# An output projection by token tiles, and an up projection in two halves of 128 tokens

## The reference

```python
y = odd_mixer(...)            # q, k, v; attention; then @ w_out_c  (1024 x 1024)
h = h + gt_m * rms_norm_2(y, g_post_m)
f = conv_ffn(modulate(h, g_pre_f, sh_f, sc_f), w_up, conv_w, conv_b, w_down)
h = h + gt_f * rms_norm_2(f, g_post_f)

def conv_ffn(x, w_up, conv_w, conv_b, w_down):
    h = x @ w_up                                   # 1024 -> 2 * 2816
    h = depthwise convolution of h over 3 tokens + conv_b
    a, g = split(h)
    return (silu(g) * a) @ w_down
```

## Time and profile before

| | |
|---|---|
| median of 3 runs | 1935.21 us (1931.68 to 1938.03) |
| profiled execution | 1930.5 us |
| its span in the trace | 1928.7 us |
| granted TensorE clock, mean | 0.996 |
| TensorE busy | 1884.9 us, 98% of the span |
| VectorE busy | 1281.4 us, 66% |
| ScalarE busy | 916.3 us, 48% |

### The profile page before, as it was taken

The page is one execution under the profiler, slowest core; times in us unless marked ns, Lnnn a source line. Parts: engine busy times, 40 slices in busy tenths (PEclk is TensorE's granted clock), DMA queues, the critical chain, the costliest instruction groups (busy, mean ns, idle before and its releaser), DMA issues.

```text
span 1928.7 us, 28546 instructions
## 1 busy us (share of the span) xinstructions
PE 1884.9 (98%) x11806; PEld 1621.3 (84%) x11806; DVE 1281.4 (66%) x1658; ACT 916.3 (48%) x1289; POOL 251.0 (13%) x174
## 2 busy tenths in 40 slices
PE   7999989999999999999999999999999999979998
PEld 6888969888888888888889878988888889679997
DVE  5776796776677768777664464755554367757774
ACT  5334565334533455633464265533433255755553
POOL 0000007842756600000000110000000000000000
PEclk9999999999999999999999999999999999999999
DMA  7775537776577642776452221323222313025452
GB/s 280 262 267 213 177 124 264 275 267 226 197 257 288 220 173 94 280 276 248 154 186 88 109 78 66 110 89 119 88 94 103 106 69 129 15 88 175 175 196 88
DMA packets 50960, 323.78 MB, mean 168 GB/s; under 512 B 5472, under 2 KB 9744, under 8 KB 12816
## 3 DMA queue, kind: packets, MB, share of 16 engines
q1 hardware_dynamic: 39024, 270.09, 38.9%
q10 hardware_dynamic: 10080, 39.28, 5.4%
q0 software_dynamic: 1728, 12.58, 1.7%
HBM read 320.86 MB, written 1.07 MB: 167 GB/s over the span
## 4 chain that ended last, share of the span: by engine, by line
PE 85%; DVE 9%; ACT 3%; issue 2%; DMA 0%; ACTq 0%; DVEq 0%
PE ps L553 83%; DVE s_wl L1937 3%; ACT s_wh L1266 1%; DVE s_tmp L2036 1%; DVE s_big L2228 1%; PE ps L906 1%; DVE s_xx L1937 1%; PE ps L763 0%; PE ps L740 0%; DVE s_tmp L2054 0%; ACT s_big L1436 0%; DVE s_tmp L2450 0%; DVE s_X L2426 0%; DVE s_X L2123 0%; DVE s_big L2059 0%
## 5 line engine op out<-in xcount | busy, mean ns | idle before, releaser
L553 PE MATMUL ps<-s_xx,s_wh 128*128 128x512 f32 (+1 forms) x3328 | 895.8, 347 | 11.2 <-DVE s_wl L2007 9.9
L1937 DVE TENSOR_TENSOR s_wl<-s_raw,s_wh 128x2048 fp32r<-128x2048 f32 x213 | 492.2, 2312 | 289.9 <-ACT s_wh L1266 289.7
L553 PE MATMUL ps<-s_xx,s_wl 128*128 128x256 f32 (+1 forms) x2208 | 668.5, 303 | 0.4 <-DVE s_xx L2453 0.4
L553 PEld LDWEIGHTS ps<-s_xx,s_wh 128*128 128x128 f32 x3328 | 579.7, 190 | 98.4 <-DVE s_wl L2007 10.3
L1266 ACT ACTIVATE s_wh<-s_raw 128x2048 fp32r<-128x2048 f32 x213 | 403.9, 1906 | 113.3 <-PE ps L553 105.9
L553 PEld LDWEIGHTS ps<-s_xx,s_wl 128*128 128x128 f32 x2208 | 419.1, 190 | 19.5 <-issue 2.7
L553 PE MATMUL ps<-s_wh,s_hl 128*128 128x512 f32 (+1 forms) x608 | 232.0, 382 | 1.6 <-DVE s_tmp L2036 0.8
L553 PE MATMUL ps<-s_wh,s_hh 128*128 128x512 f32 (+1 forms) x608 | 230.1, 378 | 0.0
L553 PE MATMUL ps<-s_wl,s_hh 128*128 128x512 f32 (+1 forms) x608 | 229.9, 378 | 0.0
L553 PE MATMUL ps<-s_wh,s_xx 128*128 128x256 f32 x928 | 178.9, 286 | 0.0
L1380 ACT ACTIVATE s_tmp<-s_tmp 128x512 f32<-128x512 f32 x44 | 27.8, 632 | 298.4 <-DVE s_tmp L2054 298.4
(11 more groups left out here) (234 smaller groups left out, 1848.3 us busy)
## 6 DMA issues: line engine op xcount, KB each, us to landing
s_raw<-in_ffn_down SPq DMA_DIRECT2D x44, 1024.0 KB, 4.8
s_raw<-in_w_up SPq DMA_DIRECT2D x44, 1024.0 KB, 4.8
s_raw<-in_ffn_gate SPq DMA_DIRECT2D x43, 1024.0 KB, 4.8
s_raw<-in_ffn_up SPq DMA_DIRECT2D x43, 1024.0 KB, 4.8
s_big<-in_w_ada ACTq DMA_DIRECT2D x34, 1024.0 KB, 6.4
s_raw<-in_w_down SPq DMA_DIRECT2D x22, 1024.0 KB, 4.7
s_raw<-in_w_in SPq DMA_DIRECT2D x18, 1024.0 KB, 4.8
s_X<-in_w_ada POOLq DMA_DIRECT2D x12, 1024.0 KB, 7.0
```

Of the source, the lines that this page charges most:

```text
L553: return pe.matmul(o, lhsT, rhs, start=start, stop=stop, skip_group_check=True)
L1937: dve.tensor_tensor(wide(wl, u), raw[:, u % SLOTS, :].rearrange("p (k n) -> p k n", k=8), f32(wide(wh, u)), SUB).then_inc(*w_low.tick(u))
```

## The change

The planner gives the unit w_out_c 3 and all later ones a fourth place, the context half of `xx`. `out_tiles` replaces `out_proj` for this layer: all four units for token tile 0, then all four for token tile 1. A bank now holds 512 columns of one token tile. The norms, with new functions on ScalarE (`tile_...`) and VectorE (`tile_...`), go tile by tile, and `turn_tile` transposes one tile; that of tile 0 is issued within the product of unit 2 for tile 1. The conversions of w_up 22 and w_up 33 stand between them. The first up unit is multiplied by `first_up` in two halves of 128 tokens, which are the moving operand, each half behind the transposes of its tile. `conv_ffn` begins with w_up 33 then. `bound_turn` before `conv_ffn` is gone.

```diff
@@ planner @@
+            if u == unit["w_out_c", 3]:
+                last[3] = unit["w_qkv", 5]
+            p = min(range(4 if u < four and name != "w_out" or u >= unit["w_out_c", 3] else 3),
+                    key=lambda n: last.get(n, -1))
@@ tensor @@
+            def turn_tile(t):
+                B = ("m", 1, 0)
+                for k in range(8):
+                    if k % 2 == 0:
+                        claim(4 + k // 2)
+                        pe.wait_ge(*normed[norm_of(B), t + 2 * (k // 4)])
+                    m = pe.transpose(turned_tile(t, k), Ys[0][:, t, 128 * k:128 * k + 128], const("ident"))
...
+            def first_up(t):
+                u = unit["w_up", 22]
+                pe.wait_ge(*w_low[u])
...
+                for k in range(8):
+                    pe.wait_ge(*x_low[norm_of(("m", 1, 0)), t, k // 2])
+                    for c in range(2):
+                        m = mm3(ps[conv_first[1][0][0]][:, 256 * c + 128 * t:256 * c + 128 * t + 128],
+                                *w_cols(u, k, 128 * c, 128), *x_cols(k, 128 * t, 128), k + c == 0, k == 7)
...
+            def out_tiles():
+                for t in range(2):
+                    for j in range(4):
+                        u, bank = unit["w_out_c", j], 2 * t + j // 2
+                        pe.wait_ge(*w_low[u])
...
+                        for k in range(8):
...
+                            if (t, j, k) == (1, 2, 4):
+                                turn_tile(0)
+                            hi, lo_ = x_cols(k, 128 * t, 128)
+                            W, L = w_cols(u, k, 0, 256)
+                            m = mm3(ps[bank][:, 256 * (j % 2):256 * (j % 2) + 256], hi, lo_, W, L, k == 0, k == 7)
...
+                first_up(0)
+                turn_tile(1)
+                first_up(1)
@@ scalar @@
-                for j in range(4):
-                    bound_squares(B, j, j)
-                    if j < 3:
-                        high_after(unit["w_out_c", j])
-                bound_root(B, 0)
-                stream_squares(B)
-                bound_root(B, 1)
-                bound_high(B, pre_ffn(1), 0, 1, 2, 3)
+                tile_squares(0, 0)
+                tile_squares(0, 1)
+                tile_root(0, 0)
+                tile_stream(0)
+                tile_root(0, 1)
+                high_after(unit["w_out_c", 0])
+                tile_squares(1, 0)
+                high_after(unit["w_out_c", 1])
+                tile_high(0)
+                tile_squares(1, 1)
+                tile_root(1, 0)
+                tile_stream(1)
+                tile_root(1, 1)
+                tile_high(1)
+                high_after(unit["w_out_c", 2])
                 high_after(unit["w_out_c", 3])
@@ vector @@
-                for j in range(3):
-                    bound_evict(B, j, j)
-                    low_after(unit["w_out_c", j])
-                bound_sum(B, 0)
-                bound_evict(B, 3, 3)
-                bound_resid(B)
-                bound_norm(B)
-                bound_low(B, pre_ffn(1), 0, 1, 2, 3)
+                def tile_low(t):
+                    for p in range(4):
+                        ...
+                        for c in range(2):
+                            ...
+                            dve.tensor_scalar(part[:, c, :], turned_tile(t, 2 * p + c), A, S, MUL, ADD)...
+                        ...
+                        dve.tensor_tensor(xl[:, 2 * p:2 * p + 2, at], part, f32(xh[:, 2 * p:2 * p + 2, at]), SUB)...
...
+                tile_evict(0, 0)
+                tile_sum(0, 0)
+                tile_evict(0, 1)
+                tile_resid(0)
+                tile_norm(0)
+                low_after(unit["w_out_c", 0])
+                tile_evict(1, 0)
+                low_after(unit["w_out_c", 1])
+                tile_low(0)
+                tile_sum(1, 0)
+                tile_evict(1, 1)
+                tile_resid(1)
+                tile_norm(1)
+                tile_low(1)
+                low_after(unit["w_out_c", 2])
                 low_after(unit["w_out_c", 3])
```

More of the change, by code:

```diff
@@ L264, in bound, with tile_bound, turned_tile @@
             return bcol[:, q, a:z]
+        def tile_bound(what, t):
+            if what in ("y", "x"):
+                return bound(0, what)[:, {"y": 4, "x": 2}[what] * t:{"y": 4, "x": 2}[what] * t + 2]
+            return bound(0, what)[:, t:t + 1]
+        def turned_tile(t, k):
+            return ps[4 + k // 2][:, 256 * (k % 2) + 128 * t:256 * (k % 2) + 128 * t + 128]
         def norm_of(B):
@@ L1101, in conv_ffn @@
                 for n, q in enumerate(streams):
-                    for i in range(2):
+                    for i in range(l, 2):
                         u = unit["w_up", 22 * l + 11 * i]
@@ L1119, in conv_ffn @@
                 conv_down(s, l, streams, down_aside)
+            def turn_tile(t):
[5 more added lines that the diff above has]
+                    m = pe.transpose(turned_tile(t, k), Ys[0][:, t, 128 * k:128 * k + 128], const("ident"))
+                    if k % 2:
+                        m.then_inc(*product.tick((norm_of(B), "turn", t, k // 2)))
+                        freed[4 + k // 2] = x_low[norm_of(B), t, k // 2]
@@ new lines, in first_up @@
+            def first_up(t):
+                u = unit["w_up", 22]
+                pe.wait_ge(*w_low[u])
+                if t == 0:
+                    claim(conv_first[1][0][0])
+                for k in range(8):
[3 more added lines that the diff above has]
+                                *w_cols(u, k, 128 * c, 128), *x_cols(k, 128 * t, 128), k + c == 0, k == 7)
+                if t:
+                    m.then_inc(*product.tick((("conv", 1), "up", 0, 0, 0)))
+                    product.also(("unit", u))
@@ new lines, in out_tiles @@
+            def out_tiles():
+                B = ("m", 1, 0)
+                for t in range(2):
+                    for j in range(4):
+                        u, bank = unit["w_out_c", j], 2 * t + j // 2
+                        pe.wait_ge(*w_low[u])
+                        if j % 2 == 0:
+                            claim(bank)
+                        for k in range(8):
+                            if t == 0 and j == 0:
+                                pe.wait_ge(*x_low["odd", "o", k])
+                            if (t, j, k) == (1, 2, 4):
[3 more added lines that the diff above has]
+                            m = mm3(ps[bank][:, 256 * (j % 2):256 * (j % 2) + 256], hi, lo_, W, L, k == 0, k == 7)
+                        m.then_inc(*product.tick((B, "part", t, j)))
+                        if t:
+                            product.also(("unit", u))
+                        if j % 2:
+                            product.also((B, "y", t + j - 1))
+                            freed[bank] = y_out[B, t + j - 1]
+                first_up(0)
+                turn_tile(1)
+                first_up(1)
@@ L1200, in odd @@
                     attend(H, n)
-                out_proj(1, "w_out_c", (0,), [[[x_low["odd", "o", k]] for k in range(8)]], {})
+                out_tiles()
             C = ("pre", 0, 1)
@@ L1238, in tensor @@
             odd()
-            bound_turn(("m", 1, 0), 0, 1, 2, 3)
             conv_ffn(1, (0,), {}, {})
@@ new lines, in tile_root, with tile_stream @@
+                def tile_root(t, n):
+                    act.wait_ge(*summed[B, n, t])
+                    act.activation(tile_bound(("root", n), t), tile_bound(("sum", n), t), ACT.Sqrt, bias=v("eps6"),
+                                   scale=1.0 / 1024).then_inc(*rooted.tick((B, n, t)))
+                def tile_stream(t):
+                    for h in range(2):
+                        b = t + 2 * h
+                        act.wait_ge(*resid[(*B, b)])
+                        act.wait_ge(*squared[B, "y", b])
+                        act.activation(T(b), half_of(Xs[0], b), ACT.Square,
+                                       accum_out=tile_bound("x", t)[:, h:h + 1]).then_inc(*squared.tick((B, "x", b)))
@@ new lines, in tile_high @@
+                def tile_high(t):
+                    for k in range(8):
+                        A, S = pre_ffn(1)(k, 0)
+                        act.wait_ge(*product[norm_of(B), "turn", t, k // 2])
+                        act.activation(xh[:, k, 128 * t:128 * t + 128], turned_tile(t, k), ACT.Identity, bias=S,
+                                       scale=A).then_inc(*x_high.tick((norm_of(B), t, k // 2)))
+                tile_squares(0, 0)
+                tile_squares(0, 1)
+                tile_root(0, 0)
@@ new lines, in tile_sum, with tile_over @@
+                def tile_sum(t, n):
+                    dve.wait_ge(*squared[B, "yx"[n], t + 2])
+                    dve.tensor_reduce(tile_bound(("sum", n), t), tile_bound("yx"[n], t), AX, ADD).then_inc(
+                        *summed.tick((B, n, t)))
+                def tile_over(t, n):
+                    dve.wait_ge(*rooted[B, n, t])
```

(16 more changed lines are left out.)

27 lines of the change are left out of this document (26 added, 1 removed).

## The result

The changed kernel takes 1938.28 us (median of 19 runs, 1935.26 to 1945.12), the kernel before 1932.15 in the same number of runs. The ratio is 1.0029 with a 95% interval of 1.0021 to 1.0037: 5.6 us slower, with 4.1 to 7.1 as the bounds. The forecast was no change (-0.1 us).

The account below looks back on a forecast made before the run. TensorE, busy 98% of the span, was taken as the bound; the first up unit's end moves from 1738.5 to 1738.35, so 1935.2 - 0.1 = 1935.1 us, range 1931 to 1944.

Parts of the forecast that it names:

- The likeliest case: First up unit: weight-bound halves of 5.76 us each, chains as forecast, shift -0.1 us, from -1.4 to +3.1; chance 0.54.
- granted clock 1.00 throughout: TensorE around the first up unit: expected sign that the clock stays at its full level through the new gaps.
- rival (c): New gaps around tile 1's transposes: the clock falls once more for 3.9 us, +0.8 to +2.1, taken as +1.5; chance 0.07.
- Rival (a): First up unit's halves: slow mode under 256 columns, 0.23 us per multiplication, +8.4 us; chance 0.20.
- The disputed price: First up unit's halves: a multiplication of 128 moving columns taken at 0.12 us, adding 5.76 us of TensorE work.
- 2-column float32 row: Earlier trace: float32 multiplications with 2 moving columns still take 0.116 us; nearest row for the price of 128 columns.
- (b): First up unit's halves: cheap multiplications at 0.067 us, the second half ending at 1736.7, -1.8 us; chance 0.14.
- The chains: ScalarE and VectorE order per tile: TensorE starts tile 0's half at 1722.45 and tile 1's at 1732.6.
- Projection, fourth place, what stands behind: Output projection 23.0 us with unit 3 in time; later work unaffected, nothing for the fourth place to gain there.
- The idle time is nearly filled, but with the 5.8 us of added multiplications: TensorE around the first up unit: one 7 us wait becomes 0.7, 1.8 and 1.7, with 5.8 us more work.

Follow-up runs that it names:

- e3_filled: Changed kernel with 9 multiplications of 512 columns before the transposes of tile 1 and 7 behind them, filling idle TensorE time: ratio 0.9996 to the kernel before.
- e4_dense: Changed kernel whose second half multiplies all 256 tokens, so its 48 multiplications have 256 moving columns: ratio 1.0010 to the kernel before.
- e7_split: Kernel before with four up and gate units in the middle of the last layer split into multiplications of 128 moving columns: ratio 1.0101 to the kernel before.
- e2_place: Kernel before with only the fourth place for w_out_c 3 and all later units: ratio 1.0003 to the kernel before.
- e9_late_whole_filled: Changed kernel, w_up 33's low part behind tile_low(1), last gap filled, 22 dummy multiplications replacing the first half, first up unit whole: ratio 0.9984 to before.
- e11_dense_then_gap: Changed kernel with the first half replaced by 24 multiplications of 512 columns, gaps kept, first up unit whole: ratio 1.0011 to the kernel before.
- e1_whole: Changed kernel with the first up unit multiplied whole, 256 moving columns, behind the transposes of both tiles: ratio 1.0012 to the kernel before.
- e6_late_whole: Changed kernel with the low part of w_up 33 behind tile_low(1) and the first up unit whole, no fillers: ratio 0.9998 to the kernel before.
- e5_late: Changed kernel with VectorE's low part of w_up 33 moved behind tile_low(1): ratio 1.0012 to the kernel before.
- e12_one_gap: Changed kernel with 9 multiplications of 512 columns before the transposes of tile 1, the gap behind them left: ratio 1.0002 to the kernel before.

## Why the prediction was wrong

- **The step that failed** is the clock. The likeliest case had it at "granted clock 1.00 throughout" and gave no reason why new gaps of 1.8 and 1.7 us should leave it there. A fall stood only in rival (c), "The clock falls once more", with a chance of 0.07 and too small a price: "for as long as it did, 3.9 us from 1730.0", "+0.8 to +2.1, I take +1.5". It is what happens. The clock fell in the idle 1.92 us before 1730.29, and came back at 1746.7, 16.4 us after the transposes began and not 3.9. Loss by it: 6.5 us (e3_filled), of which the likeliest case had none. Two things were misread. In the earlier trace rows the clock had been down not for 3.9 us but for 6.8: the mean of 0.79 over the 7.10 us of idle time is another 3.0 us at half, a fall about 4 us after the last multiplication. In the changed kernel 1.3 us were enough, which no row of before showed. And the earlier trace rows went on with 256 columns behind the gap; the return was taken as a matter of time and not of the work that follows. e4_dense separates the two.
- **Luck.** The measured median of 1938.28 lies just inside the 1933.8 to 1938.3 of the likeliest case. But these were counted from 1935.21, the median of three runs of the kernel before, and 19 runs give 1932.15. The shift is +5.6, outside that case's -1.4 to +3.1. Rival (a) names +5.5 us for a price just over 0.20; there both halves would have been slow, here the first took 0.111 and the second 0.213, so that nearness says nothing for (a).
- **The disputed price** was right: 0.12 forecast, 0.111 measured. The 2-column float32 row was the right neighbour. The Trainium skill, page "TensorE: Matmul & The Clock Gate", section "LDWEIGHTS (loading the stationary operand)", gives the load of P columns of weights as P/1.2 ns; that is an estimate of 107 ns for 128 columns, and the measured 0.111 agrees with it. The same page of the Trainium skill, section "Back-to-back issue gap", names about 81 ns for 128 columns in a stream; for this type the traces show 111, so the measurement decides. Rivals (a) at 0.23 and (b) at 0.067 are both excluded, by the after trace and by e7_split.
- **The chains** were right within about 0.5 us. Forecast, with the 0.8 us by which the marks differ added: the first half at 1723.2 (1722.82), sum of tile 1 at 1726.4 (1725.89), transposes at 1730.8 (1730.29), second half at 1733.4 (1733.24). With the clock held, e3_filled ends at -0.81 in the trace where -0.1 was forecast; 0.4 of it is the 0.111 instead of 0.12, and the second half starts 0.4 earlier than forecast.
- **Projection, fourth place, what stands behind**: no wait for w_out_c 3 (198 multiplications in the 23.3 us of the projection and the transposes), e2_place at +0.02, and 173.00 of 173.00 us busy behind. All as forecast.
- **"The idle time is nearly filled, but with the 5.8 us of added multiplications"** was the right reading of what the halves do, and e9_late_whole_filled shows it: dummy multiplications do as well, to 0.2 us.

## What to carry to other kernels

When a change cuts one long idle gap of TensorE into short ones, don't count the clock as won: an idle time of 1.9 us brought it down here (changed kernel, e4_dense), and so did two of 2.1 and 1.6 us with eight transposes between them (e11_dense_then_gap). What followed decided how long it stayed down. Splitting the moving columns from 256 to 128 saved next to no time per multiplication (0.111 for 128 columns, 0.120 for 256) and cost double behind a fall (0.213) until the 256-column work came. Price the clock in each stretch behind a gap, and try dummy multiplications in the gap: they are a cheap way to see what the clock is worth.

## What was not expected of the hardware

- Ten microseconds of multiplications without a break, each of 128 columns, did not bring the clock back from 1.2 to 2.4 GHz (1733.24 to 1743.51 in the changed kernel), though TensorE counted as busy for all of them. With 256 columns it was back 3.0 us (e1_whole), 3.3 (e4_dense) and 3.6 (e6_late_whole) after the unit began, and 5.5 in e11_dense_then_gap, where the unit began 1.4 us after the fall.
- The same thin multiplications kept the full clock for over 40 us when no gap came before them (e7_split).
- The clock can fall in the middle of busy work, 1.7 us after it resumed (e5_late, at about 1734.4 after a start at 1732.67). In e12_one_gap, with an idle time as long in the same place, it held in the one trace. What exactly sets the moment is not settled here.
